# Expert rows written by plain scatters into a table of two rows for each token, in a two-layer hybrid step with 32 experts

## The chip, the cores and the metric

The kernel runs on one core of one Trainium2 chip. The metric is the device time of one execution in microseconds (us), given as the median over runs.

## What is computed

The program is one inference step of two trunk layers (an mLSTM and attention layer, then a state-space and delta-rule layer) over 128 prompt and 256 sample tokens of width 1024, all float32. Each layer ends in a mixture of experts, and only that part is touched by the change. Each of the T = 384 tokens chooses one of four expert groups, and two of the 8 experts in it. The result for a token is the sum of its two experts' outputs, each with its weight:

```
gsel = argmax(glog);  elog = elog[group gsel]
tv, ti = lax.top_k(elog, 2);  tw = softmax(tv) * gprob[gsel]
act_e = silu(x @ w_gate[e]) * (x @ w_up[e]) * combine[:, e]
y = sum over e of act_e @ w_down[e]
```

The reference evaluates all 32 experts on all tokens. Since the combine weights are zero but for two experts a token, 768 rows of expert output (2 x 384) carry all of the result.

## The kernel before

The five engines run programs written by hand, tied by named semaphores; S("name") is one. Work of TensorE (PE) stands in a fixed list of jobs, each with one of eight PSUM banks. computed(job) is the wait for its bank to be full, taken(job) the wait for it to be read.

**The expert stage** of a layer is gathered(l). Each expert has 64 slots (CAP), two experts share a pair of 128 slots, and there is one more pair with two spare blocks of 64, for experts that got over 64 tokens. That makes 17 pairs (PAIRS); the spare pair is the ninth in order (SPARE_AT = 8). For each pair, in the order of time:

- SyncE (SP) loads the weights of the two experts by 4 transfers of 1 MB for gate and up (load_pair, L595) and 2 of 1 MB for down (L600). There are two buffers. The gate and up weights of pair n are asked for when the gate-up products of pair n-2 are done, the down weights when its down products are done.
- GpSimd (POOL) gathers the tokens' rows by an indirect DMA from the DRAM table h_rows (gather, L736). The list of rows is slot_token, one column of 128 row numbers for each pair; an empty slot holds 512, which is out of bounds and moves nothing.
- PE turns the rows (L1167), ScalarE (ACT) copies them to SBUF (L1605), and PE multiplies them with gate and up (gate_up, L1180, 32 matmuls), 64 slots to each half of the array. ACT and VectorE (DVE) form silu(gate) * up (L1613, L2111), PE turns that (L1191), DVE copies it (L2115), and PE multiplies by down (L1205, 16 matmuls).
- ACT scales columns 0 to 511 of the result by the slots' weights (L1621), DVE columns 512 to 1023 (L2120), into one of two buffers yrow.
- POOL adds the 128 rows of yrow to the DRAM table y_rows of the layer by an indirect DMA with compute_op=ALU.add (scatter, L749). The row is the token's number, so that a token's two results meet in one row, in two different transfers. Each scatter waits until the one before has landed (semaphore gathered_scattered, L748). The spare pair's two blocks may hold the same token, so they go in two such transfers, with the lists spare_rows, which POOL copies out of slot_token ahead of the first gather (L756).

The tables y_rows, (T, D) for each layer, are filled with zeros near the start of the program by POOL (L719), after its list of small loads.

**Where the lists come from.** The router's tail on DVE makes hot_pair, which has a 1 where choice w of a token lies in pair q, and hot_row, which has a 1 at the slot within the pair. Products of the two on PE (slot_lists, L1140) give for each slot the token's number (hot_value 0, L2078) and its weight (hot_value 1, L2079). DVE writes them out as slot_token (L2084) and share (L2085). The bank is released by a small memset (L2087).

**The end of the stage.** SP waits for the last scatter, and reads the table back as three tiles of 128 tokens (ysel, L648, semaphores chosen0_in to chosen2_in). PE waits for all three and turns them by 24 transposes (L1262), after which DVE adds them to the residual (L1983). SP's next work, the weights of the second layer, stands behind the wait for the third tile. If more experts overflow than the spare blocks can hold, a dense path under overflow() runs all experts; it isn't taken here.

Of the kernel before, what the change touches and what calls it, by code (L numbers as in the profile page):

```python
# [90 lines left out]
C_ALL = C_TOKEN + TILES  # L91
NOWHERE = 512


def const_table():
# [21 lines left out]
    c[:, C_TOKEN:C_TOKEN + TILES] = row + P * np.arange(TILES)[None, :] - NOWHERE  # L117
    for parity in range(2):
        for half in range(2):
            for cond in range(2):  # L120
                c[32 * (2 * parity + half) + cond, C_SEL + 2 * parity + cond] = 1.0
# [126 lines left out]
def build(nc, a, o):  # L248
# [7 lines left out]
    with es:  # L256
# [12 lines left out]
        y_dram = [nc.dram_tensor(f"y_rows{l}", (T, D), F32).ap() for l in range(2)]  # L269
# [40 lines left out]
        pair_slot = cst[:, C_FIRST:C_FIRST + PAIRS + 1]  # L310
        iota, token = cst[:, C_IOTA:C_IOTA + P], cst[:, C_TOKEN:C_TOKEN + TILES]
# [8 lines left out]
        def scatters(l, n):  # L320

            return (PAIRS + 1) * l + n + 1 + (n >= SPARE_AT)
# [26 lines left out]
        spare_rows = sb("spare_rows", [P, 2], I32)  # L349
# [17 lines left out]
        def carve(n, at=None):  # L367
# [26 lines left out]
        act_n = [carve(FF) for _ in range(2)]  # L394
        act_s = [carve(2 * P).rearrange("p (j s) -> p j s", j=2) for _ in range(2)]
# [7 lines left out]
        hot_value = act_s[0].rearrange("p j s -> p (j s)")[:, 0:2 * TILES * 2 * PAIRS].rearrange(  # L403
            "p (w c n q) -> p w c n q", w=2, c=TILES, n=2)
        used[0] = base + 3 * 2 * T
        used[0] = max(used[0], work_end)
        ysel = carve(TILES * D).rearrange("p (c d) -> p c d", c=TILES)
# [123 lines left out]
        def _(sp):  # L531
# [92 lines left out]
            def moe(l):  # L624
# [21 lines left out]
                sp.wait_ge(S("gathered_scattered"), 16 * scatters(l, PAIRS - 1))  # L646
                for c in range(TILES):
                    sp.dma_start(ysel[:, c], y_dram[l][c * P:(c + 1) * P, :]).then_inc(S(f"chosen{c}_in"), 16)  # L648
# [10 lines left out]
            sp.wait_ge(S(f"chosen{TILES - 1}_in"), 16)  # L659
# [6 lines left out]
        def _(pool):  # L666
# [9 lines left out]
            with nc.allow_non_contiguous_dma(reason="small vectors"):  # L676
# [38 lines left out]
                last_token = pool.to_reg(T - 1)  # L715
# [1690 lines left out]
```

## Time and profile before

| | us |
|---|---|
| median of 3 runs | 1636.43 |
| the three runs | 1626.86, 1636.43, 1638.61 |
| the profiled execution | 1630.42 |
| its span | 1628.6 |
| PE busy | 1323.0 (81% of the span) |
| DVE, ACT, POOL busy | 522.8, 343.9, 153.8 |
| DMA, all queues | 335.48 MB, mean 206 GB/s |

The span is the time from the first to the last instruction, and the profiled execution is 1.8 us longer than that. PE is the busiest engine on the average, but the average mixes stages in which PE is the limit with stages in which it waits for weights. A row of the timeline gives start, duration, engine, line, operation and tiles, and in brackets the idle time ahead of it with what ended it. "issue" there means that the engine waited for something that the profile doesn't resolve to an instruction. A row of the windows gives for one stretch the busy time of each engine with its count of instructions, the TensorE clock that was granted (1.00 is 2.4 GHz, 0.50 is 1.2 GHz), the mean busy share of the 16 DMA engines, and the rate in GB/s. In the DMA view, q1 is the queue that SP issues to and q0 the one that POOL issues to; a row gives packets, MB, and the time that the packets took as a share of 16 engines over the stretch.

### The profile page before, as it was taken

What the parts mean: (1) busy time and instruction counts of PE and PEld (TensorE: products, weight loads), DVE (VectorE), ACT (ScalarE), POOL (GpSimd) and SP (SyncE); (2) the same over time, 40 slices, a digit from 0 to 9 for tenths busy, and PEclk for the clock granted to TensorE, in tenths of its full rate; (3) what the DMA queues carried; (4) which work ended last, traced back from release to release, by engine and by line L of the source; (5) the groups of instructions that cost most, each with busy time, mean ns of one, the idle gap of its engine ahead of it and who ended that gap; (6) DMA issues with size and microseconds to landing.
All of it is one profiled execution on the core that took longest, in us unless ns stands there. A gap on an engine that the chain in (4) does not pass through costs nothing.

```text
span 1628.6 us, 16057 instructions
## 1 busy us (share of the span) xinstructions
PE 1323.0 (81%) x6198; PEld 804.6 (49%) x6198; DVE 522.8 (32%) x1060; ACT 343.9 (21%) x720; POOL 153.8 (9%) x151
## 2 busy tenths in 40 slices
PE   5999899777977887877599997888869597878763
PEld 3545684344873333322366557787859533323223
DVE  3011662222242010000356816677741610000103
ACT  2100313322221111111326213222231211111102
POOL 2300000000011111110000010000000211111110
PEclk8999889877887998999799998999979699989986
DMA  9923555254444999997523200000033589999932
GB/s 338 320 71 120 190 172 207 89 221 155 181 177 185 409 412 406 396 397 279 163 73 134 76 3 1 27 1 1 1 122 163 206 312 409 406 402 397 391 148 78
DMA packets 81538, 335.48 MB, mean 206 GB/s; under 512 B 19160, under 2 KB 20354, under 8 KB 55217
## 3 DMA queue, kind: packets, MB, share of 16 engines
q1 hardware_dynamic: 67088, 309.94, 48.3%
q0 software_dynamic: 14368, 24.44, 5.8%
q8 instruction: 53, 0.87, 0.2%
q14 instruction: 29, 0.23, 0.0%
HBM read 329.96 MB, written 28.48 MB: 220 GB/s over the span
## 4 chain that ended last, share of the span: by engine, by line
PE 70%; DVE 14%; issue 10%; DMA 2%; ACT 2%; POOL 0%; SPq 0%; DVEq 0%; ACTq 0%; POOLq 0%
PE psum L867 19%; PE psum L1180 17%; PE psum L959 8%; PE psum L1205 8%; PE psum L891 3%; PE psum L1167 2%; PE psum L954 2%; DVE arena L2226 1%; DVE mix L2186 1%; PE psum L1080 1%; PE psum L1060 1%; PE psum L910 1%; PE psum L898 1%; PE psum L1191 1%; DVE arena L2115 1%
## 5 line engine op out<-in xcount | busy, mean ns | idle before, releaser
L1180 PE MATMUL psum<-arena 128*64 128x512 f32 x576 | 145.8, 664 | 41.6 <-issue 39.2
L1180 PE MATMUL psum<-ring,arena 128*64 128x512 f32 x512 | 134.1, 683 | 41.7 <-issue 41.7
L867 PE MATMUL psum<-hT,ring 128*128 128x384 f32 x448 | 150.9, 500 | 7.0 <-ACT hT L1461 5.1
L2111 DVE TENSOR_TENSOR arena<-arena,psum 128x256 f32<-128x256 f32 x34 | 14.3, 421 | 358.8 <-ACT arena L1613 358.8
L959 PE MATMUL psum<-ring 128*128 128x128 f32 x872 | 114.0, 289 | 18.4 <-issue 9.1
L867 PEld LDWEIGHTS psum<-hT,ring 128*128 128x128 f32 x448 | 87.5, 196 | 69.1 <-issue 12.1
L959 PEld LDWEIGHTS psum<-ring 128*128 128x128 f32 x872 | 108.2, 202 | 23.6 <-issue 13.8
L1180 PEld LDWEIGHTS psum<-arena 128*64 128x64 f32 x576 | 50.0, 153 | 136.2 <-issue 133.0
L867 PE MATMUL psum<-ring,hT 128*128 128x512 f32 (+2 forms) x336 | 116.4, 508 | 0.0
L1180 PEld LDWEIGHTS psum<-ring,arena 128*64 128x64 f32 x512 | 45.7, 157 | 129.8 <-issue 129.8
L1613 ACT ACTIVATE arena<-psum 128x256 f32<-128x256 f32 x34 | 13.0, 384 | 390.5 <-PE psum L1180 390.5
L867 PE MATMUL psum<-mix,ring 128*128 128x384 f32 x256 | 92.2, 517 | 0.0
L749 POOL DMA_INDIRECT y_rows<-arena,slot_token x32 | 50.6, 1582 | 416.7 <-DVE arena L2120 392.2
L867 PEld LDWEIGHTS psum<-ring,hT 128*128 128x128 f32 x336 | 58.5, 191 | 57.2 <-issue 56.4
L867 PEld LDWEIGHTS psum<-mix,ring 128*128 128x128 f32 x256 | 79.5, 316 | 6.3 <-issue 4.2
L1205 PE MATMUL psum<-arena 128*64 128x512 f32 x288 | 65.8, 598 | 9.3 <-DVE arena L2115 9.3
L2120 DVE TENSOR_SCALAR arena<-psum,share 128x512 f32<-128x512 f32 x34 | 25.5, 751 | 127.8 <-PE psum L1205 127.8
L1205 PE MATMUL psum<-ring,arena 128*64 128x512 f32 x256 | 58.5, 598 | 8.3 <-DVE arena L2115 8.3
L891 PE MATMUL psum<-ring,sil 128*32 128x512 f32 x384 | 57.3, 747 | 6.0 <-issue 6.0
L727 POOL TENSOR_TENSOR mix<-mix,arena 128x1024 f32<-128x1024 f32 x6 | 14.1, 2366 | 503.6 <-ACT mix L1595 503.6
L1983 DVE SCALAR_TENSOR_TENSOR xT<-psum,modT,xT 128x128 f32<-128x128 f32 x64 | 23.7, 413 | 109.1 <-PE psum L867 80.1
L2226 DVE SCALAR_TENSOR_TENSOR arena<-arena,colsT 128x388 f32<-128x388 f32 x80 | 49.8, 623 | 2.8
(475 smaller groups left out, 1654.7 us busy)
## 6 DMA issues: line engine op xcount, KB each, us to landing
ring<-in_ada_w SPq DMA_DIRECT2D x24, 2048.0 KB, 10.9
arena<-in_moe_w_gate SPq DMA_DIRECT2D x36, 1024.0 KB, 11.8
arena<-in_moe_w_up SPq DMA_DIRECT2D x36, 1024.0 KB, 14.3
arena<-in_moe_w_down SPq DMA_DIRECT2D x36, 1024.0 KB, 17.4
ring<-in_moe_w_gate SPq DMA_DIRECT2D x32, 1024.0 KB, 12.0
ring<-in_moe_w_up SPq DMA_DIRECT2D x32, 1024.0 KB, 17.9
ring<-in_moe_w_down SPq DMA_DIRECT2D x32, 1024.0 KB, 18.7
ring<-in_w_in_odd SPq DMA_DIRECT2D x7, 2048.0 KB, 7.9
```

The costliest lines, as they stand in the source:

```text
L749: pool.indirect_dma_start(out=y_dram[l], out_offset=bass.IndirectOffsetOnAxis(ap=where.bitcast(U32), axis=0), in_=yrow[u], in_offset=None, ...
L867: ins = mm(out, lhs(k), rhs(k), start=(k == 0), stop=(k == n - 1))
L891: ins = mm(b[at_:at_ + 32, :], sil[:, 4 * half + k, :], w[half][:, k, parity::2], start=(k == 0), stop=(k == 3), tile_position=(0, at_))
L898: ins = mm(b[:, 4 * m:4 * m + 4], mod_rows[:, m::4], pick, start=True, stop=True)
L954: ins = mm(b[:, tok(h)], col(h).to_broadcast([P, P]), ident, start=True, stop=True)
L959: ins = mm(b[:, h * width:(h + 1) * width], lhs(h), rhs(h), start=True, stop=True)
L1167: ins = nc.tensor.transpose(psum[:, k // 4, tok(k % 4)], hrow[q % 2][:, tok(k)], ident)
L1180: ins = mm(psum[half, 2 + s, :].rearrange("p (w f) -> p w f", w=2), hg[s][:, k, half], pair_gu[s][h][:, :, k, :], start=(k == 0), stop=(k ...
L1205: ins = mm(psum[half, 5 + n, :], act_s[s][:, j, half], pair_dn[s][h][:, j, 512 * n:512 * n + 512], start=(j == 0), stop=(j == 1), tile_pos ...
L1983: ins = stt(xT[:, m, t0:t1], bank(name, l, m)[:, t0:t1], modT[:, l, part, m, j:j + 1], xT[:, m, t0:t1], ALU.mult, ALU.add)
L2120: ts(yrow[q % 2][:, 512:D], psum[:, 6, :], share[:, ORDER[q]:ORDER[q] + 1], None, ALU.mult).then_inc(S(f"{kind}yb"), 1)
L2226: ins = stt(conv[:, i, :], cin[:, i, w:w + COUT], wcol[w], conv[:, i, :], ALU.mult, ALU.add)
```

## The change

The DRAM table y_rows of a layer gets two rows for each token, (2 * T, D): row token for its first choice, row T + token for its second. No two slots of any pair then write to the same row, and so the scatters no longer add and no longer wait for each other; each has a column of a new list, slot_row. The spare pair goes in one transfer like the others, and the copies into spare_rows are gone. slot_row comes from a third row of hot_value (one more DVE operation, and 51 columns in place of 34 in the product), with the constants C_ROW. It is written by a DVE operation that takes the place of the memset which released the bank. Scatters count on two semaphores, by the parity of the pair. At the end SP reads six tiles back, two for each 128 tokens. DVE adds the two tiles of each 128 tokens, and PE waits for these three sums. The zero fill is of twice as many rows.

```
-        y_dram = [nc.dram_tensor(f"y_rows{l}", (T, D), F32).ap() for l in range(2)]
+        y_dram = [nc.dram_tensor(f"y_rows{l}", (2 * T, D), F32).ap() for l in range(2)]
...
+    c[:, C_ROW:C_ROW + 2 * TILES] = row + P * np.arange(2 * TILES)[None, :] - NO_ROW
...
-            return (PAIRS + 1) * l + n + 1 + (n >= SPARE_AT)
+            return (PAIRS + 1 - n % 2) // 2 * l + n // 2 + 1
...
+        used[0] = base + 3 * 2 * T
+        ysel.append(carve(TILES * D).rearrange("p (c d) -> p c d", c=TILES))
...
-                sp.wait_ge(S("gathered_scattered"), 16 * scatters(l, PAIRS - 1))
+                for n in range(PAIRS - 2, PAIRS):
+                    sp.wait_ge(S(f"gathered_scattered{n % 2}"), 16 * scatters(l, n))
                 for c in range(TILES):
-                    sp.dma_start(ysel[:, c], y_dram[l][c * P:(c + 1) * P, :]).then_inc(S(f"chosen{c}_in"), 16)
+                    for w in range(2):
+                        at = w * T + c * P
+                        sp.dma_start(ysel[w][:, c], y_dram[l][at:at + P, :]).then_inc(S(f"chosen{c}_in"), 16)
...
-            sp.wait_ge(S(f"chosen{TILES - 1}_in"), 16)
+            sp.wait_ge(S(f"chosen{TILES - 1}_in"), 32)
...
-                    pool.dma_start(y_dram[l].rearrange("(p n) d -> p n d", p=P), bc(zero_row, 1, [P, T // P, D]))\
+                    pool.dma_start(y_dram[l].rearrange("(p n) d -> p n d", p=P), bc(zero_row, 1, [P, 2 * T // P, D]))\
...
+                        if n == 0:
+                            pool.wait_ge(*taken("ix", l))
                         pool.wait_ge(S("gathered_ya"), PAIRS * l + n + 1)
                         pool.wait_ge(S("gathered_yb"), PAIRS * l + n + 1)
-                        for i in range(2 if n == SPARE_AT else 1):
-                            where = spare_rows[:, i:i + 1] if n == SPARE_AT else slot_token[:, q:q + 1]
-                            if n + i:
-                                pool.wait_ge(S("gathered_scattered"), 16 * (scatters(l, n - 1) + i))
-                            pool.indirect_dma_start(
-                                out=y_dram[l], out_offset=bass.IndirectOffsetOnAxis(ap=where.bitcast(U32), axis=0),
-                                in_=yrow[u], in_offset=None, bounds_check=last_token,
-                                oob_is_err=False, compute_op=ALU.add).then_inc(S("gathered_scattered"), 16)
-
-                    for i in range(2):
-                        part = slice(CAP * i, CAP * i + CAP)
-                        nc.gpsimd.tensor_copy(spare_rows[part, i:i + 1], slot_token[part, PAIRS - 1:PAIRS]).then_inc(S("spare_rows"), 1)
-                    pool.wait_ge(S("spare_rows"), 2 * l + 2)
+                        pool.indirect_dma_start(
+                            out=y_dram[l], out_offset=bass.IndirectOffsetOnAxis(ap=slot_row[:, q:q + 1].bitcast(U32), axis=0),
+                            in_=yrow[u], in_offset=None, bounds_check=last_row,
+                            oob_is_err=False).then_inc(S(f"gathered_scattered{u}"), 16)
...
-                for c in range(TILES):
-                    pe.wait_ge(S(f"chosen{c}_in"), 16 * (l + 1))
+                pe.wait_ge(S("chosen_added"), TILES * (l + 1))
...
-                o_(tt(hot_value[:, :, :, 1, :], hot_pair, bc(wt, 3, each), ALU.mult))
+                tt(hot_value[:, :, :, 1, :], hot_pair, bc(wt, 3, each), ALU.mult)
+                o_(tt(hot_value[:, :, :, 2, :], hot_pair, bc(y_at, 3, each), ALU.mult))
...
-                take(v.memset(nbm, 0.0), "ix", l)
+                take(ts(slot_row[:], bank("ix", l)[:, 2 * PAIRS:3 * PAIRS], float(NO_ROW), None, ALU.add), "ix", l)
...
+                for c in range(TILES):
+                    dve.wait_ge(S(f"chosen{c}_in"), 32 * (l + 1))
+                    done(tt(ysel[0][:, c, :], ysel[0][:, c, :], ysel[1][:, c, :], ALU.add), "chosen_added")
```

On POOL, where the lists are ready and the first gathers go out, this stands before (the rows' add of shifts ends with L727, L736 is a gather):

```order
L727 TENSOR_TENSOR mix<-mix,arena 128x1024 [waits bank3_read,bank2_read]
L756 COPY spare_rows<-slot_token 64x1 [waits h_rows_out,rows_clear,slots,rows_zero]
L756 COPY spare_rows<-slot_token 64x1
L736 DMA arena<-h_rows,slot_token 128x1024 [waits spare_rows]
L736 DMA arena<-h_rows,slot_token 128x1024
```

and this after, where gathers are on L745 and scatters on L756:

```order
L736 TENSOR_TENSOR mix<-mix,arena 128x1024 [waits bank3_read,bank2_read]
L745 DMA arena<-h_rows,slot_token 128x1024 [waits h_rows_out,rows_clear,slots,rows_zero]
L745 DMA arena<-h_rows,slot_token 128x1024
L745 DMA arena<-h_rows,slot_token 128x1024 [waits gathered_turned]
L756 DMA y_rows<-arena,slot_row 768x1024 [waits gathered_yb,gathered_ya,bank6_read]
```

The two copies and the wait for them are gone, the first gather now stands right behind the waits for the list, and the first scatter waits for the bank that slot_row is read from.

On POOL, around the spare pair of the first layer, this stands before:

```order
L749 DMA y_rows<-arena,slot_token 384x1024 [waits gathered_scattered,gathered_yb,gathered_ya]
L736 DMA arena<-h_rows,slot_token 128x1024 [waits gathered_turned]
L749 DMA y_rows<-arena,spare_rows 384x1024 [waits gathered_scattered,gathered_yb,gathered_ya]
L749 DMA y_rows<-arena,spare_rows 384x1024 [waits gathered_scattered]
L736 DMA arena<-h_rows,slot_token 128x1024 [waits gathered_turned]
L749 DMA y_rows<-arena,slot_token 384x1024 [waits gathered_scattered,gathered_yb,gathered_ya]
```

and this after:

```order
L745 DMA arena<-h_rows,slot_token 128x1024 [waits gathered_turned]
L756 DMA y_rows<-arena,slot_row 768x1024 [waits gathered_yb,gathered_ya]
L745 DMA arena<-h_rows,slot_token 128x1024 [waits gathered_turned]
L756 DMA y_rows<-arena,slot_row 768x1024 [waits gathered_yb,gathered_ya]
L745 DMA arena<-h_rows,slot_token 128x1024 [waits gathered_turned]
```

One of the two transfers of the spare pair and every wait for an earlier scatter are gone; the order of gathers and scatters is the same.

On SP, at the end of the stage, where y_rows is read back, this stands before:

```order
L600 DMA arena<-in_moe_w_down 128x2048 [waits gathered_y1_computed]
L600 DMA arena<-in_moe_w_down 128x2048
L648 DMA arena<-y_rows 128x1024 [waits gathered_scattered]
L648 DMA arena<-y_rows 128x1024 x2
L527 TENSOR_LOAD flag [waits flag]
L527 ISA x2
L527 COMPARE_AND_BRANCH
```

and this after:

```order
L606 DMA arena<-in_moe_w_down 128x2048 [waits gathered_y1_computed]
L606 DMA arena<-in_moe_w_down 128x2048
L657 DMA arena<-y_rows 128x1024 [waits gathered_scattered0,gathered_scattered1]
L657 DMA arena<-y_rows 128x1024 x5
L533 TENSOR_LOAD flag [waits flag]
L533 ISA x2
L533 COMPARE_AND_BRANCH
```

Three loads have become six, in front of the same test for the overflow. On DVE, at the end of the router, this stands before (L2082 makes hot_row):

```order
L2076 SCALAR_TENSOR_TENSOR slots_f<-slots_f 128x6
L2078 TENSOR_TENSOR arena<-arena,cst 128x6x17
L2079 TENSOR_TENSOR arena<-arena,slots_f 128x6x17
L2082 TENSOR_SCALAR arena<-cst,slots_f 128x128 x6
L2084 TENSOR_SCALAR slot_token<-psum 128x17
L2085 COPY share<-psum 128x17
L2087 MEMSET small 128x2
```

and this after, where L2084 makes hot_row:

```order
L2077 SCALAR_TENSOR_TENSOR slots_f<-slots_f 128x6
L2079 TENSOR_TENSOR arena<-arena,cst 128x6x17
L2080 TENSOR_TENSOR arena<-arena,slots_f 128x6x17
L2081 TENSOR_TENSOR arena<-arena,cst 128x6x17
L2084 TENSOR_SCALAR arena<-cst,slots_f 128x128 x6
L2086 TENSOR_SCALAR slot_token<-psum 128x17
L2087 COPY share<-psum 128x17
L2089 TENSOR_SCALAR slot_row<-psum 128x17
```

One operation more stands ahead of the six that make hot_row, and the memset has become the one that writes slot_row.

## Rows read from the trace of the kernel before

**Rows 1.** The page's 40 slices of the span: DMA share in tenths.

```profile
DMA  9923555254444999997523200000033589999932
```

**Rows 2.** The chain that ended last, first layer's expert stage: start, us, what.

```profile
576.80 2.48 issue
579.27 8.75 PE psum L1180 x32
```

**Rows 3.** The same chain, end of that stage.

```profile
779.16 6.21 DMA y_rows<-arena,slot_token
...
785.75 0.43 SPq L648
786.23 5.17 DMA arena<-y_rows
...
791.64 5.36 PE psum L1262 x24
```

**Rows 4.** Windows of the first layer's expert stage.

```profile
512.30:540.00 27.70, 25.80 (x128) 10.29 (x130) 4.04 (x8) 5.60 (x8) 5.29 (x4) 1.00 0.98 385
...
574.00:608.00 34.00, 28.07 (x120) 10.60 (x118) 3.19 (x6) 4.19 (x6) 5.25 (x4) 0.90 1.02 409
```

**Rows 5.** Gate-up products (L1180) in the timeline of PE, first layer.

```profile
518.12 7.04 PE L1180 MATMUL psum<-ring,arena 128*64 128x512 f32 x32
...
530.61 7.04 PE L1180 MATMUL psum<-arena 128*64 128x512 f32 x32
...
562.66 8.52 PE L1180 MATMUL psum<-arena 128*64 128x512 f32 x32 [5.62 <-issue]
...
748.83 9.30 PE L1180 MATMUL psum<-ring,arena 128*64 128x512 f32 x32 [5.16 <-issue]
```

**Rows 6.** DMA queues, 512.3 to 748.8 us: packets, MB, share of 16 engines.

```profile
q1 hardware_dynamic: 12300, 89.63, 91.3%
q0 software_dynamic: 4176, 5.16, 8.7%
```

**Rows 7.** The same, second layer, 1311.3 to 1549 us.

```profile
q1 hardware_dynamic: 12297, 89.60, 90.7%
q0 software_dynamic: 4176, 4.96, 8.7%
```

**Rows 8.** POOL's queue while it moves gathers alone, 496 to 502 us.

```profile
q0 software_dynamic: 288, 0.32, 20.4%
...
arena<-h_rows,slot_token POOLq DMA_INDIRECT x3, 3.9
```

**Rows 9.** POOL's queue, 779 to 785.4 us, the last scatter of the first layer.

```profile
q0 software_dynamic: 144, 0.36, 41.3%
```

**Rows 10.** POOL's queue, 1447 to 1456 us, a spare block's scatter.

```profile
q0 software_dynamic: 144, 0.01, 1.6%
```

**Rows 11.** DMA issues of the whole span: KB each, us to landing.

```profile
y_rows<-arena,slot_token POOLq DMA_INDIRECT x32, 9.3
...
out_gdn<-arena POOLq DMA_DIRECT2D x2, 256.0 KB, 3.3
```

**Rows 12.** Timeline at the start of the stage.

```profile
491.58 0.26 DVE L2079 TENSOR_TENSOR arena<-arena,slots_f 128x102 f32<-128x102 f32 x1
...
495.09 0.18 DVE L2084 TENSOR_SCALAR slot_token<-psum 128x17 int32<-128x17 f32 x1 [1.95 <-PE psum L1140]
...
496.20 1.10 POOL L736 DMA_INDIRECT arena<-h_rows,slot_token  x1 [0.38 <-POOL spare_rows L756]
```

**Rows 13.** SP's queue, 785.3 to 791.5 us, y_rows read back.

```profile
q1 hardware_dynamic: 432, 1.57, 66.1%
```

**Rows 14.** An addition of 128x1024 on DVE, by form.

```profile
L2190 DVE TENSOR_TENSOR arena<-arena,mix 128x1024 f32<-128x1024 f32 x1 | 1.2, 1215 | 0.0
```

**Rows 15.** Windows around the zero fill.

```profile
66.00:81.00 15.00, 15.00 (x48) 8.82 (x47) 0.00 (x0) 1.47 (x3) 0.00 (x0) 1.00 1.00 390
81.00:90.00 9.00, 9.00 (x29) 5.16 (x28) 0.00 (x0) 0.98 (x2) 0.00 (x0) 1.00 0.03 10
```

More of the change, by code:

```diff
@@ L90 @@
 C_TOKEN = C_IOTA + P
-C_ALL = C_TOKEN + TILES
-NOWHERE = 512
+C_ROW = C_TOKEN + TILES
+C_ALL = C_ROW + 2 * TILES
+NOWHERE, NO_ROW = 512, 1024
 def const_table():
@@ L310, in build @@
         pair_slot = cst[:, C_FIRST:C_FIRST + PAIRS + 1]
+        y_at = cst[:, C_ROW:C_ROW + 2 * TILES].rearrange("p (w c) -> p w c", w=2)
         iota, token = cst[:, C_IOTA:C_IOTA + P], cst[:, C_TOKEN:C_TOKEN + TILES]
@@ L348, in build @@
         share = sb("share", [P, PAIRS])
-        spare_rows = sb("spare_rows", [P, 2], I32)
+        slot_row = sb("slot_row", [P, PAIRS], I32)
         spare_id = sb("spare_id", [1, 2, SPARE], I32)
@@ L394, in build @@
         act_n = [carve(FF) for _ in range(2)]
+        act_at = used[0]
         act_s = [carve(2 * P).rearrange("p (j s) -> p j s", j=2) for _ in range(2)]
@@ L713, in _ @@
                 zero_row = route[:].rearrange("p a c n -> p (a c n)")[:, 0:D]
-                last_token = pool.to_reg(T - 1)
+                last_token, last_row = (pool.to_reg(n - 1) for n in (T, 2 * T))
                 pool.wait_ge(S("zeroed"), 1)
                 for l in range(2):
-                    pool.dma_start(y_dram[l].rearrange("(p n) d -> p n d", p=P), bc(zero_row, 1, [P, T // P, D]))\
+                    pool.dma_start(y_dram[l].rearrange("(p n) d -> p n d", p=P), bc(zero_row, 1, [P, 2 * T // P, D]))\
                         .then_inc(S("rows_zero"), 16)
@@ L1139, in slot_lists @@
                     w_, c = n // TILES, n % TILES
-                    ins = mm(b[:, 0:2 * PAIRS], hot_row[:, w_, c, :], hot_value[:, w_, c].rearrange("p n q -> p (n q)"),
+                    ins = mm(b[:, 0:3 * PAIRS], hot_row[:, w_, c, :], hot_value[:, w_, c].rearrange("p n q -> p (n q)"),
                              start=(n == 0), stop=(n == 2 * TILES - 1))
@@ L1261, in moe @@
                     for c in range(TILES):
-                        ins = nc.tensor.transpose(b[:, tok(c)], ysel[:, c, m::KD], ident)
+                        ins = nc.tensor.transpose(b[:, tok(c)], ysel[0][:, c, m::KD], ident)
                     ready(ins)
@@ L1619, in gathered @@
                     if q >= 2:
-                        act.wait_ge(S(f"{kind}scattered"), 16 * scatters(l, q - 2))
+                        act.wait_ge(S(f"{kind}scattered{q % 2}"), 16 * scatters(l, q - 2))
                     fn(yrow[q % 2][:, 0:512], psum[:, 5, :], ACT.Copy, scale=share[:, ORDER[q]:ORDER[q] + 1]).then_inc(S(f"{kind}ya"), 1)
@@ L1754, in _ @@
             o_(v.memset(eps[:], EPS))
-            o_(v.memset(spare_rows[:], OOB))
             o_(v.memset(crowded[:, :, EXPERTS:EXPERTS + 1], 0.5))
@@ L2118, in gathered @@
                     if q >= 2:
-                        dve.wait_ge(S(f"{kind}scattered"), 16 * scatters(l, q - 2))
+                        dve.wait_ge(S(f"{kind}scattered{q % 2}"), 16 * scatters(l, q - 2))
                     ts(yrow[q % 2][:, 512:D], psum[:, 6, :], share[:, ORDER[q]:ORDER[q] + 1], None, ALU.mult).then_inc(S(f"{kind}yb"), 1)
@@ L2149, in dense @@
                 for c in range(TILES):
-                    dve.wait_ge(S(f"chosen{c}_in"), 16 * (l + 1))
-                    done(tt(ysel[:, c, :], ysel[:, c, :], yacc[:, c, :], ALU.add), f"{kind}merged")
+                    dve.wait_ge(S(f"chosen{c}_in"), 32 * (l + 1))
+                    done(tt(ysel[0][:, c, :], ysel[0][:, c, :], yacc[:, c, :], ALU.add), f"{kind}merged")
             def before_experts(l):
@@ L2171, in moe @@
                     dense(l)
+                for c in range(TILES):
+                    dve.wait_ge(S(f"chosen{c}_in"), 32 * (l + 1))
+                    done(tt(ysel[0][:, c, :], ysel[0][:, c, :], ysel[1][:, c, :], ALU.add), "chosen_added")
             before_experts(0)
```

6 lines of the change are left out of this document (3 added, 3 removed).

## Prediction

> **What bounds the kernel now.** I read the page's slices first: DMA stands at 9 tenths in two plateaus, the expert stages of the two layers [rows 1]. The page's busy times would point to PE, with 81% of the span, but the chain of waits in the plateau alternates between PE's products and gaps that the profile calls "issue" [rows 2]. What PE waits for there is told by the windows: the DMA share is 0.98 from 512.3 to 540 us and 1.02 from 574 to 608, at about 400 GB/s, two of seven windows in a row up to 744 us, which lie between 0.98 and 1.02 [rows 4]. The third check is the distance between pairs. Two early pairs whose weights were loaded ahead are 12.49 us apart (530.61 - 518.12). From pair 4 to pair 15, eleven steps later, it is (748.83 - 562.66) / 11 = 16.92 us [rows 5]. Where the granted clock of the window is 0.90, one pair's gate-up products take 8.75 us [rows 2]; where it is 1.00, 7.04 us [rows 4, 5]. So PE alone would need 12.49 + 1.7 = 14.2 us. So from gu_computed of the first pair (512.3 us) to the weights of pair 15 (748.8 us) the stage is as long as the work of the 16 DMA engines. The second layer has the same form, from 1311.3 to 1549 us [rows 7]. The last two pairs run at PE's own pace. Behind them stands a serial tail in which PE and DVE are idle: the last scatter takes 6.21 us from its issue to landing, the read-back some 6 us from its issue, and then come the 24 transposes [rows 3].
>
> So there are three places where this change can count: the DMA work of the plateau, the tail, and the start of the stage.
>
> **The plateau: adding against plain writes.** In the window 512.3 to 748.8 us (236.5 us), SP's queue moved 89.63 MB in 91.3% of the engines' time, that is 215.9 us, or 2.41 us for each MB [rows 6]. POOL's queue took 8.7%, or 20.6 us, for 5.16 MB; at 2.41 us for each MB those would be 12.4 us. The excess of 8.1 us is what small packets and the adding cost. The small packets are priced where POOL's queue moves almost no bytes: 144 packets took 1.6% of 9 us, 0.14 us, of which some 0.05 us are its 0.01 MB, so 0.1 us for about 141 small ones [rows 10]. The window has 4176 packets, of which 5.16 MB / 4096 B = 1260 are rows, so 2916 small ones, 2.0 us. That leaves 6.1 us for the adding. The second layer by the same steps (237.7 us): 215.6 us for 89.60 MB, 20.7 us for 4.96 MB, excess 8.8 us, less 2.1 us, 6.7 us [rows 7]. Two isolated stretches say the same in another way: gathers alone took 20.4% of 6 us for 0.32 MB, 3.8 us for each MB; the last scatter alone 41.3% of 6.4 us for 0.36 MB, 7.3 us for each MB [rows 8, 9]. An added row costs about two plain ones. Half of the 5.16 MB are scattered, 2.5 MB, so this second way gives (7.3 - 3.8) x 2.5 = 8.8 us. No row before shows an indirect plain write, so I keep 0 and 8.8 us for each layer as ends, and take 6.1 and 6.7, since they come from the busy window itself. Since the engines are full there, time that they save is time that the stage saves: 16.92 - 6.1 / 14, or 16.5 us a pair, is still over PE's 14.2. Sum: **-12.8 us**. The waits between scatters that go were not on the path: a scatter lands 9.3 us after its issue [rows 11], in a pair of 17 us. The second transfer for the spare pair is worth 0.14 us a layer, in the rounding.
>
> **The start.** slot_token is ready at 495.27 us, the first gather is issued at 496.20, behind the two copies [rows 12]; the 0.93 us fall to perhaps 0.15. One DVE operation of the form of L2079, 0.26 us, is added ahead of hot_row [rows 12], and 17 more columns in the product. The plateau starts from the first pair's products, so this counts: -0.8 + 0.3, -0.5 us for each layer (ends -0.9 and +0.3): **-1.0 us**. slot_row takes the memset's place, behind slot_token, beside the gather; behind the new wait of the first scatter (for the bank) only POOL's next gather is queued, and the bank is read some 20 us earlier.
>
> **The tail.** The last scatter: 6.21 us before [rows 3]. Its plain form has the nearest rows in a gather with 3.9 us [rows 8] and in plain writes to DRAM from POOL in a quiet stretch, 3.3 us [rows 11]. Ends: 3.3 and 6.2. I take 4.4, near the gather and somewhat over it since it is a write with a list: -1.8 us for each layer, **-3.6 us**. The Trainium skill ("DMA: Bandwidth & Descriptors", section "Anatomy of one DMA — SWDGE (gpsimd) path") says that a DMA from GpSimd has about 2 us of fixed time, mostly the receipt of its last write, and the rest goes by bytes. By that rule only the packets' own time would shrink, from 2.64 us to 1.4, so 1.3 us a layer in place of 1.8, and the sum would be -5.6 us; no row of before shows which holds.
>
> The read-back doubles: 432 packets took 66.1% of 6.2 us, 4.1 us for 1.57 MB [rows 13]. SP issues a load in 0.43 us [rows 3], less than the 1.3 us that 0.52 MB takes, so the bytes count in full: +4.1 us a layer, **+8.2 us** (ends 3.3 and 4.5 each). Then the sum of the last tile: an addition of 128x1024 takes 1.2 us [rows 14] with 0.1 for the semaphore, while the first two are done under the loads: +1.3 a layer, **+2.6 us**. Nothing hides this pair of terms, since PE waits for all three sums and SP's weights for the next layer for the loads. Those weights come 2.3 us later, against a chain that is 3.6 us later before they are needed, so they cost nothing more.
>
> **The zero fill** moves 3.1 MB more, 7.6 us of all engines at 2.41 us for each MB. It stands behind the small loads on its queue, and after it the engines are nearly idle: share 0.03 from 81 to 90 us, while PE is busy in all of both windows [rows 15]. These 8.7 free us take it, so 0; with that cover gone it would be 7.6 us, once.
>
> **Sum.** -12.8 - 1.0 - 3.6 + 8.2 + 2.6 = -6.6 us. The span goes from 1628.6 to 1622.0, the profiled execution from 1630.4 to 1623.8. The median of the runs is 6.0 us over the profiled execution, and the runs spread over 11.8 us, twice the effect. I set the number off the mean of the four executions shown, 1633.1: 1626.5, rounded to 1627.
>
> **Rivals.**
>
> *The adding is nearly free, and row traffic as such is the cost.* If a packet of a scattered row takes its time because of the list and the two ends in different memories, the plateau keeps its length, and so does the last scatter. Then the doubled read-back and the sums decide: -1.0 + 8.2 + 2.6 = +9.8 us, 1643: slower than before. The point is where the plateau and the last scatters together save less than 9.8 us. For it: POOL's queue takes more per MB in gathers too, 3.8 us against SP's 2.41 [rows 6, 8]. Against it: the ratio of 1.9 between scatter and gather in isolated stretches [rows 8, 9].
>
> *PE takes the bound.* If with shorter waits the granted clock stays at its lower level for more pairs, PE's pace of 14.2 us a pair would still be below 16.5, so some of the gain at most is lost in the pairs behind the last weights, where a gate-up product takes 9.30 or 7.04 us [rows 5]. Some 2 us a layer: net -2.6 us, 1631.
>
> *All ends fall well.* Plateau -17.6, start -1.8, last scatters -5.8, read-back +6.6, sums +2.4: -16.2 us, 1617. For it: the second way of pricing. Against it: that way takes scatters in an idle stretch, where an engine also waits for answers from memory.
>
> *The zero fill isn't hidden*: +7.6 us on top of the forecast, net +1.0, 1634. Against it stands the free stretch [rows 15].
>
> **How the numbers follow.** Forecast (net -12 to -3 us) 0.55; PE's clock takes a part 0.12; all ends well 0.13; adding nearly free 0.12; zero fill 0.08. A measurement of this kernel can tell about 1%, 16 us, from no change. Only the case of good ends comes near that on the fast side, and the spread of the runs can carry it over; the slow side needs two of the bad cases at once. Faster by over 1%: 0.11, within 1%: 0.84, slower: 0.05. The range takes in the cases and the runs' spread: 1616, just under the good ends, 1642 for nearly the rival on the slow side. The forecast's own range, as medians go, is 1620 to 1632.
>
> **What would show it.** In the plateau POOL's queue should take 6% of the engines' time in place of 8.7 at the same MB, and both plateaus should be 6 to 7 us shorter, at a DMA share still near 1.0 and pairs 16.5 us apart. The last scatter should land in 4 to 5 us. From the read-back's issue to its landing it should take some 10 us, then one addition of 1.2 us, then the transposes. The stretch from 81 to 89 us should be full of writes with PE still busy. The prediction is wrong if the plateau keeps its length, or if the DMA share falls well below 1 in it (another limit took over), or if PE waits for weights between 90 and 110 us.

## The result: 1637.5 us before, 1616.7 us after

With three more runs the median of the kernel before is 1637.52 us (6 runs), and that of the changed kernel is 1616.65 us (1612.7 to 1621.15, 6 runs). The ratio is 0.9874, with a 95% interval from 0.9845 to 0.9904. The forecast was 1627 with a net gain of 6.6 us. The time lies inside the range given (1616 to 1642) by 0.65 us, but the gain is 20.9 us, three times the forecast, and beyond its own range (1620 to 1632). That it landed inside is luck more than insight: the forecast gave a gain of over 1% a chance of 0.11, and the gain is 1.3%. It also started from 1633.1 us, the mean of the four executions at hand, and the median of six is 1637.5. The profiled execution takes 1612.70 us with a span of 1610.9, against 1630.42 and 1628.6: 17.7 us less.

Where the 17.7 us went is read from a few marks in the two traces. The plateau is counted here from the start of the first pair's gate-up products to the start of pair 15's. "Read-back" runs from SP's first issue to the start of PE's transposes.

| us | before, layer 0 and 1 | after, layer 0 and 1 | change | forecast |
|---|---|---|---|---|
| up to the first pair | 502.8 | 503.7 | +0.9 | -0.5 |
| plateau | 246.0, 246.1 | 234.9, 234.9 | -22.3 | -12.8 |
| pair 15 to the last scatter's issue | 30.3, 32.1 | 29.7, 29.7 | -3.0 | 0 |
| last scatter, issue to SP's next issue | 6.2, 5.9 | 4.0, 3.5 | -4.6 | -3.6 |
| read-back, and the addition after | 6.3, 6.7 | 11.7, 11.8 | +10.5 | +10.8 |
| transposes to the next layer's first pair | 511.3 | 512.4 | +1.0 | -0.5 |
| after the last transposes' start | 34.8 | 34.6 | -0.2 | 0 |

One row carries most of the difference of 11.1 us: the plateaus gained 9.5 us more. The tail came out nearly as forecast.

The two stretches ahead of the plateaus (2.9 us over the forecast together) and the last pairs (3.0 us under it) cancel. Of the 1.9 us that those two stretches grew, 0.88 and 1.03 us lie ahead of the first operation that the edit touches, L2078 before and L2079 after (491.39 and 1290.96 us before, 492.27 and 1284.37 after). What comes so early moves from one execution to the next: in three executions of the changed kernel the first pair starts at 503.7, 508.1 and 510.2 us.

The gate-up products in the timeline of PE, changed kernel, first layer (the rows for comparison are [rows 5]):

```profile
503.74 9.12 PE L1183 MATMUL psum<-arena 128*64 128x512 f32 x32 [1.17 <-ACT arena L1607]
...
543.70 7.04 PE L1183 MATMUL psum<-ring,arena 128*64 128x512 f32 x32
...
560.34 9.82 PE L1183 MATMUL psum<-arena 128*64 128x512 f32 x32 [3.99 <-issue]
```

and for the end of the plateau:

```profile
738.63 8.78 PE L1183 MATMUL psum<-ring,arena 128*64 128x512 f32 x32 [2.52 <-issue]
...
754.10 7.09 PE L1183 MATMUL psum<-arena 128*64 128x512 f32 x32 [1.08 <-issue]
```

Pair 3 no longer waits at all (7.04 us with no bracket), and from pair 4 to pair 15 the distance is (738.63 - 560.34) / 11 = 16.21 us, where it was 16.92.

Windows of the changed kernel in the plateau, with the columns of [rows 4]:

```profile
540.00:574.00 34.00, 28.76 (x126) 10.63 (x128) 3.35 (x7) 4.52 (x7) 4.04 (x4) 0.90 1.02 422
574.00:608.00 34.00, 27.83 (x126) 10.56 (x122) 3.94 (x7) 4.88 (x7) 4.04 (x4) 0.95 1.01 422
...
676.00:710.00 34.00, 28.89 (x126) 10.88 (x124) 3.20 (x6) 4.19 (x6) 4.04 (x4) 0.90 1.00 412
```

The DMA share is what it was, the rate is 422 GB/s in place of 409. DMA still sets the pace, with more weights in the same time. The DMA queues in the first plateau of the changed kernel, 512.8 to 738.6 us (before: [rows 6]):

```profile
q1 hardware_dynamic: 12181, 88.77, 94.2%
q0 software_dynamic: 4032, 5.15, 6.3%
```

and in the second, 1305 to 1531.2 us (before: [rows 7]):

```profile
q1 hardware_dynamic: 12175, 88.72, 94.1%
q0 software_dynamic: 4032, 4.95, 6.0%
```

POOL's queue takes 6.3% and 6.0% for 5.15 and 4.95 MB, where it took 8.7%. That is the 6% that the forecast named: 14.2 us in place of 20.6 in the first layer, 6.4 us less. Yet the plateau is 11.1 us shorter. The share is a mean over 16 engines, and the mean doesn't hold the whole saving. Nor does a mean of 1.0 say that no engine idles: windows with 1.02 show more packet time than there is time, so packets of one engine overlap in this count.

The tail of the first layer in the timeline of the changed kernel, POOL's scatter, SP's six loads, DVE's three additions, PE's transposes:

```profile
768.35 0.98 POOL L756 DMA_INDIRECT y_rows<-arena,slot_row  x1 [12.75 <-DVE arena L2122]
772.33 3.02 SPq L657 DMA_DIRECT2D arena<-y_rows  x6
777.57 1.23 DVE L2176 TENSOR_TENSOR arena<-arena 128x1024 f32<-128x1024 f32 x1 [9.98 <-DMA arena<-y_rows]
780.31 1.23 DVE L2176 TENSOR_TENSOR arena<-arena 128x1024 f32<-128x1024 f32 x1 [1.51 <-DMA arena<-y_rows]
...
782.74 1.22 DVE L2176 TENSOR_TENSOR arena<-arena 128x1024 f32<-128x1024 f32 x1 [1.20 <-DMA arena<-y_rows]
...
784.02 4.65 PE L1264 MATMUL psum<-cst,arena 128*128 128x128 f32 x24 [17.22 <-DVE arena L2176]
```

The scatter takes 3.98 us from its issue to SP's next (772.33 - 768.35), near the 4.4 taken. The loads run from 772.33 to 782.7, the last addition takes 1.22 us on the path as forecast, and the first two lie under the loads. POOL's queue from 768 to 772.3 us, the last scatter, with the columns of [rows 9]:

```profile
q0 software_dynamic: 144, 0.36, 22.1%
```

and SP's queue from 772.3 to 782.8 us, the read-back, with the columns of [rows 13]:

```profile
q1 hardware_dynamic: 864, 3.15, 79.4%
```

The scatter's packets took 22.1% of 4.3 us, 0.95 us in place of 2.64 for the same 0.36 MB; the read-back's 79.4% of 10.5 us, 8.3 us for 3.15 MB, twice 4.1.

The zero fill, windows with the columns of [rows 15]:

```profile
66.00:81.00 15.00, 15.00 (x49) 8.77 (x48) 0.00 (x0) 1.47 (x3) 0.00 (x0) 1.00 1.03 404
81.00:90.00 9.00, 9.00 (x29) 5.32 (x28) 0.00 (x0) 0.85 (x2) 0.00 (x0) 1.00 0.85 344
90.00:97.00 7.00, 7.00 (x17) 3.04 (x17) 0.55 (x1) 0.13 (x1) 0.00 (x0) 1.00 0.86 300
```

The share from 81 to 90 us is 0.85 in place of 0.03, and PE is busy in all of the three windows. The idle stretch took the fill.

The start of the stage, with the columns of [rows 12]:

```profile
492.63 0.26 DVE L2081 TENSOR_TENSOR arena<-arena,cst 128x102 f32<-128x102 f32 x1
...
496.16 0.18 DVE L2086 TENSOR_SCALAR slot_token<-psum 128x17 int32<-128x17 f32 x1 [1.98 <-PE psum L1143]
...
497.18 1.08 POOL L745 DMA_INDIRECT arena<-h_rows,slot_token  x1 [12.72 <-DVE slot_token L2086]
```

The first gather comes 0.84 us behind the end of slot_token (496.34), 0.78 us in the second layer, where it came 0.93 us behind with the two copies between. The forecast had 0.15. The first of the two copies had indeed started 0.13 us behind slot_token (495.40 against 495.27), but a gather in its place doesn't.

### The profile page after: what moved, and what is told of

Its sections match the earlier page's. It is cut to its first block, busy times and chain, and to the rows that moved or that the text cites. A ratio compares the mean times of both kernels' runs of the same rounds, so it can differ in the third digit from the quotient of the medians.

```text
span 1610.9 us, 16071 instructions
## 1 busy us (share of the span) xinstructions
PE 1317.4 (82%) x6198; PEld 804.4 (50%) x6198; DVE 530.8 (33%) x1067; ACT 343.9 (21%) x720; POOL 129.4 (8%) x145
## 4 chain that ended last, share of the span: by engine, by line
PE 70%; DVE 14%; issue 9%; DMA 2%; ACT 2%; SPq 0%; POOL 0%; DVEq 0%; ACTq 0%; POOLq 0%
PE psum L870 19%; PE psum L1183 17%; PE psum L962 8%; PE psum L1208 8%; PE psum L894 3%; PE psum L1170 2%; PE psum L957 2%; DVE arena L2231 1%; DVE mix L2191 1%; PE psum L1083 1%; PE psum L1063 1%; PE psum L901 1%; DMA arena<-y_rows 1%; PE psum L913 1%; PE psum L1194 1%
## 5 line engine op out<-in xcount | busy, mean ns | idle before, releaser
L1183 PE MATMUL psum<-arena 128*64 128x512 f32 x576 | 153.1, 692 | 45.9 <-issue 43.6
L1183 PE MATMUL psum<-ring,arena 128*64 128x512 f32 x512 | 119.8, 622 | 19.4 <-issue 19.4
L962 PE MATMUL psum<-ring 128*128 128x128 f32 x872 | 114.8, 290 | 17.7 <-issue 8.4
L870 PEld LDWEIGHTS psum<-hT,ring 128*128 128x128 f32 x448 | 88.3, 198 | 69.7 <-issue 12.8
L1208 PE MATMUL psum<-arena 128*64 128x512 f32 x288 | 65.8, 598 | 9.3 <-DVE arena L2117 9.3
L756 POOL DMA_INDIRECT y_rows<-arena,slot_row x34 | 34.1, 1003 | 459.9 <-DVE arena L2122 430.3
L1208 PE MATMUL psum<-ring,arena 128*64 128x512 f32 x256 | 58.5, 599 | 8.3 <-DVE arena L2117 8.3
L736 POOL TENSOR_TENSOR mix<-mix,arena 128x1024 f32<-128x1024 f32 x6 | 14.1, 2369 | 509.1 <-ACT mix L1597 509.1
```

Source lines behind the costliest of these rows:

```text
L756: pool.indirect_dma_start(out=y_dram[l], out_offset=bass.IndirectOffsetOnAxis(ap=slot_row[:, q:q + 1].bitcast(U32), axis=0), in_=yrow[u], ...
L870: ins = mm(out, lhs(k), rhs(k), start=(k == 0), stop=(k == n - 1))
L962: ins = mm(b[:, h * width:(h + 1) * width], lhs(h), rhs(h), start=True, stop=True)
L1183: ins = mm(psum[half, 2 + s, :].rearrange("p (w f) -> p w f", w=2), hg[s][:, k, half], pair_gu[s][h][:, :, k, :], start=(k == 0), stop=(k ...
L1208: ins = mm(psum[half, 5 + n, :], act_s[s][:, j, half], pair_dn[s][h][:, j, 512 * n:512 * n + 512], start=(j == 0), stop=(j == 1), tile_pos ...
```

## The experiments

Theory A, formed from the result and from the packets: the plateau goes at the pace of the fullest of the 16 DMA engines. It supposes that a transfer of weights gives each engine an equal part and has landed when all have done it, while the rows of a gather or a scatter aren't spread equally: the slots of an expert are filled from the first on, 24 of 64 on the average (768 rows over 32 experts), so the engines that own the first partitions of each half would carry the most rows.

The packet records of the plateau hold 1255 rows of 4096 B on POOL's queue in either kernel. Before, they fall into two groups, at 159 and at 327 ns; in the changed kernel nearly all take 159 ns. So a gathered or plainly scattered row takes 159 ns at the median, an added one 327, and by theory A the adding cost 168 ns for each row of the fullest engine, not of the mean one. Theory B keeps the forecast's mean, and puts the rest on the waits between scatters; C puts all on those waits; D says that the places of the rows don't matter.

The times of the experiments are medians; each plateau is counted as above and comes from one profiled execution. Three executions of the changed kernel have plateaus from 234.4 to 234.9 us, so a difference of 1 us says little and one of 3 us counts.

| | median us | ratio to before, 95% | plateaus us |
|---|---|---|---|
| kernel before | 1637 to 1639 | | 246.0, 246.1 |
| changed kernel | 1616.65 | 0.9874 [0.9845, 0.9904] | 234.9, 234.9 |
| e1_add_back | 1646.33 | 1.0044 [1.0016, 1.0073] | 246.3, 246.6 |
| e2_serial_back | 1617.64 | 0.9871 [0.9834, 0.9908] | 234.8, 235.6 |
| e3_spread | 1604.02 | 0.9791 [0.9753, 0.9828] | 231.2, 228.6 |
| e4_crowd | 1646.30 | 1.0051 [1.0025, 1.0077] | 249.8, 248.2 |
| c1_control | 1620.57 | 0.9895 [0.9822, 0.9967] | 234.5, 234.8 |
| e5_before_spread | 1615.22 | 0.9878 [0.9824, 0.9932] | 237.4, 235.7 |
| e6_one_table | 1609.61 | 0.9850 [0.9801, 0.9899] | 234.7, 234.4 |
| e7_no_fill | 1618.94 | 0.9900 [0.9869, 0.9931] | 234.7, 234.5 |
| e8_spread_again | 1607.33 | 0.9814 [0.9779, 0.9849] | 231.4, 229.9 |
| c2_control | 1622.05 | 0.9898 [0.9864, 0.9932] | 234.6, 234.4 |

### The adding alone, put back

```
-                            oob_is_err=False).then_inc(S(f"gathered_scattered{u}"), 16)
+                            oob_is_err=False, compute_op=ALU.add).then_inc(S(f"gathered_scattered{u}"), 16)
```

> The changed kernel with one edit: its scatters add again (compute_op=ALU.add), into rows that are zero and that nobody else writes. No wait comes back. Theory A (the fullest DMA engine sets the plateau, and an added row takes 327 ns of it where a plain one takes 159): both plateaus, from the first pair's gate-up products to the start of pair 15's, grow by some 11 us each to about 246 us, as they were before (246.0 and 246.1 against 234.9 and 234.9), and the last scatter of a layer takes some 6 us again in place of 4.0. That is about +26 us on the changed kernel's 1616.7, so 1640 to 1645, slower than the kernel before by the doubled read-back. Rival B (the adding costs its mean over 16 engines, 6.4 us a layer, and the rest of the gain came from the waits between scatters): +6 to +7 us in each plateau, 1633. Rival C (all of it came from the waits): +0 in the plateaus.

Measured: 1646.33 us, +29.7 on the changed kernel, and the plateaus back at 246.3 and 246.6 us, as long as before. In the timeline of PE of this kernel, the first pair's gate-up products:

```profile
510.11 8.90 PE L1183 MATMUL psum<-arena 128*64 128x512 f32 x32 [1.17 <-ACT arena L1607]
```

and those of pair 15, 246.34 us later:

```profile
756.45 8.61 PE L1183 MATMUL psum<-ring,arena 128*64 128x512 f32 x32 [3.56 <-issue]
```

POOL's queue in this plateau (519 to 756.4 us):

```profile
q0 software_dynamic: 4032, 5.16, 8.6%
```

The mean share is 8.6%, about as in [rows 6], where it was 8.7%. Against 6.3% in the changed kernel this prices the adding at 20.4 - 14.2 = 6.2 us, while the plateau grew by 11.4. The last scatter of the first layer takes 5.94 us, from 786.85 to SP's issue at 792.79:

```profile
786.85 1.55 POOL L756 DMA_INDIRECT y_rows<-arena,slot_row  x1 [13.04 <-DVE arena L2122]
```

The plateaus (+23.1 us) and the last scatters (about +2 each) make most of the 29.7. So the whole of the plateau's gain is the adding. B's 6 to 7 us and C's 0 are out.

### The waits alone, put back

```
+                        if n:
+                            pool.wait_ge(S(f"gathered_scattered{1 - u}"), 16 * scatters(l, n - 1))
                         pool.indirect_dma_start(
```

> The changed kernel with one edit: each scatter again waits on POOL until the one before has landed. They stay plain. Theory A: nothing, within 2 us of the changed kernel's 1616.7, since a scatter lands in some 8 us of a pair of 16 us. Rival B: +4 to +5 us in each plateau, 1626. Rival C: +11 us in each plateau, 1638.

Measured: 1617.64 us, plateaus of 234.8 and 235.6. The series in which the scatters stood cost nothing that shows: 0.7 us in one plateau, 0 in the other.

### The places of the slots

```
-    c[:, C_IOTA:C_IOTA + P] = np.arange(P)
+    slot = np.arange(P)
+    place_of = 64 * (slot // 64) + 4 * (slot % 8) + slot % 64 // 8 % 4 + 32 * (slot % 64 // 32)
+    c[:, C_IOTA + place_of] = slot
```

This is e3_spread. hot_row compares with iota, so the constant alone decides in which partition a slot's row, weight and target lie. For e4_crowd the line in the middle reads:

```
+    place_of = 64 * (slot // 64) + 4 * (slot % 64 // 8) + slot % 8 % 4 + 32 * (slot % 8 // 4)
```

> The changed kernel with one constant changed: slot r of an expert's 64 lies in another of its 64 partitions, 4 * (r % 8) + r // 8 % 4 + 32 * (r // 32), so that consecutive slots fall on eight different DMA engines, if partition p belongs to engine 8 * (p >> 6) + ((p >> 2) & 7). That is the assignment that the Trainium skill gives ("DMA: Bandwidth & Descriptors", section "The descriptor swizzle"). An expert has 24 rows on the average, and its slots are filled from the first one on, so as it stands the first engine of a half gets 4 to 8 rows of each transfer and the last often none. The routing of these inputs gives for the first 14 pairs of layer 0 and 1 at most 68 and 72 rows on one engine, at a mean of 38 and 42; the new places give 45 and 49. Theory A (the fullest engine sets the pace): 23 rows less on it, each gathered and scattered at 159 ns, 7.3 us less in each plateau, 227.5 us; 1602. Rival D (the mean over the engines sets the pace, or rows go to engines in turn): no change, 1616.7, or a few us more.

> The changed kernel with the same constant changed the other way: eight consecutive slots fall on one engine, place 4 * (r // 8) + r % 8 % 4 + 32 * (r % 8 // 4). The fullest engine then has 108 and 107 rows in the first 14 pairs in place of 68 and 72, at the same mean. Theory A: 40 and 35 rows more at 2 x 159 ns, +12.7 and +11.1 us in the plateaus, about 1640. Rival D: no change, 1616.7.

Measured: spreading gives 1604.02 us with plateaus of 231.2 and 228.6, crowding 1646.30 us with 249.8 and 248.2. The instructions, bytes and packets are the same in both. Gate-up products in the timeline of the spread kernel, of the first pair and of pair 3:

```profile
509.94 9.08 PE L1185 MATMUL psum<-arena 128*64 128x512 f32 x32 [1.17 <-ACT arena L1609]
...
549.85 7.04 PE L1185 MATMUL psum<-ring,arena 128*64 128x512 f32 x32
```

and of pair 15:

```profile
741.11 9.54 PE L1185 MATMUL psum<-ring,arena 128*64 128x512 f32 x32 [4.37 <-issue]
```

The same in the timeline of the crowded kernel, the first pair and pair 3, which waits 1.37 us here and not at all in the spread one:

```profile
506.70 8.97 PE L1185 MATMUL psum<-arena 128*64 128x512 f32 x32 [1.17 <-ACT arena L1609]
...
548.04 7.09 PE L1185 MATMUL psum<-ring,arena 128*64 128x512 f32 x32 [1.37 <-issue]
```

and pair 15:

```profile
756.53 8.65 PE L1185 MATMUL psum<-ring,arena 128*64 128x512 f32 x32 [3.08 <-issue]
```

The DMA queues in the first plateau of the spread kernel, 519 to 741.1 us:

```profile
q1 hardware_dynamic: 12041, 87.75, 94.5%
q0 software_dynamic: 4032, 5.15, 6.4%
```

and of the crowded one, 515.8 to 756.5 us:

```profile
q1 hardware_dynamic: 12364, 90.13, 91.4%
q0 software_dynamic: 4032, 5.15, 5.9%
```

POOL's 5.15 MB take 14.2 us of mean engine time in both (6.4% of 222.1, 5.9% of 240.7), and the plateaus differ by 18.7 us. D is out: the mean can't show on which engines the rows lie. The shares of both queues together are 97.3% in the crowded plateau and 100.9% in the spread one, which fits engines that idle more in the crowded one. The sizes fit A roughly. Crowding was to add 12.7 and 11.1 us and added 14.9 and 13.3; spreading was to take 7.3 each and took 3.7 and 6.3. For the part that spreading didn't bring, no run shows the cause.

The rule used for the places is the Trainium skill's ("DMA: Bandwidth & Descriptors", section "The descriptor swizzle"), which gives engine 8 * (p >> 6) + ((p >> 2) & 7) for partition p in a transfer to all 128 partitions. The signs of both runs agree with it for an indirect DMA as well, the sizes within a fifth for crowding and at half to nine tenths for spreading. The packet records don't name the engine of a packet, so the runs show that the partitions matter in this pattern, and that the limit is the DMA engine and not something else shared by the same partitions is argued.

### The same places in the kernel before

The same constant in the kernel before, with its adding scatters in series.

> The kernel before, with adding scatters in series, and only the slots' places changed as in e3_spread. Theory A (the rows on the fullest DMA engine set the plateau, an added one for 327 ns and a plain one for 159): the spread kernel's plateaus of 231.2 and 228.6 us, plus the adding on the fullest engine after spreading, 45 and 49 rows x 168 ns = 7.6 and 8.2 us: 238.8 and 236.8, in place of 246. So 7 to 9 us less in each layer than the kernel before, 1637.5 - 16 = 1621. Rival D (the mean sets the pace): no change, 1637. Rival B (the serial scatters hold something up): no change either, since the waits stay.

Measured: 1615.22 us, with plateaus of 237.4 and 235.7, against 238.8 and 236.8 expected. The first pair's gate-up products in its timeline:

```profile
510.97 8.94 PE L1182 MATMUL psum<-arena 128*64 128x512 f32 x32 [1.17 <-ACT arena L1607]
```

and those of pair 15:

```profile
748.40 9.69 PE L1182 MATMUL psum<-ring,arena 128*64 128x512 f32 x32 [4.09 <-issue]
```

One constant in the kernel before brings as much as the whole change: the intervals of the two ratios, 0.9878 and 0.9874, lie over each other. Its plateaus are 1 to 3 us longer than the changed kernel's, and its tail is shorter, as it reads one table back. It also shows that the price of the adding hangs on the places: with the slots filled from the front the adding costs 11.4 and 11.7 us (e1_add_back against the changed kernel), with the slots spread 6.2 and 7.1 us (this kernel against e3_spread, where the waits differ too, which cost nothing above). A mean over the engines has no room for that; theory A had 7.6 and 8.2 us for the spread places.

### The tail, and the fill

e6_one_table, in short:

```
-                    for w in range(2):
+                    for w in range(1):
...
-                pe.wait_ge(S("chosen_added"), TILES * (l + 1))
+                for c in range(TILES):
+                    pe.wait_ge(S(f"chosen{c}_in"), 16 * (l + 1))
...
-                    done(tt(ysel[0][:, c, :], ysel[0][:, c, :], ysel[1][:, c, :], ALU.add), "chosen_added")
```

> The changed kernel, but it reads back only the first table of each layer, three tiles, and leaves out the second experts' outputs and the three additions on DVE. This times the tail: the forecast's +4.1 us for the doubled read-back and +1.3 us for the last addition, for each layer. If they are right, the time from the last scatter's issue to PE's transposes falls from 15.67 to about 10.3 us in layer 0, and the total by 10.8 us to 1606. Rival: the loads of the second table were partly hidden, and the total falls by less than 6 us.

Measured: 1609.61 us, 11.0 us less than the control of its group (1620.57), whose four executions lie between 1606.76 and 1625.96 us, so the traces say more than this difference. The tail of the first layer in the timeline:

```profile
768.94 0.97 POOL L756 DMA_INDIRECT y_rows<-arena,slot_row  x1 [12.09 <-DVE arena L2123]
773.41 1.28 SPq L657 DMA_DIRECT2D arena<-y_rows  x3
...
780.11 5.20 PE L1265 MATMUL psum<-cst,arena 128*128 128x128 f32 x24 [12.73 <-DMA arena<-y_rows]
```

From the last scatter's issue to the transposes it is 780.11 - 768.94 = 11.17 us, 4.5 less than 15.67. From SP's first issue alone it is 6.70 us, 5.0 less than 11.69. In the second layer the time from pair 15 to the transposes falls from 45.0 us (46.5 in the control) to 39.7, by 5.4 at least. The forecast had 5.4 us a layer for the second table and its addition; measured are 4.5 and 5.4 in the profiled executions, and 5.5 a layer in the medians. The rival, loads of the second table that were partly hidden, had under 6 us in both layers together and is out.

e7_no_fill:

```
-                for l in range(2):
-                    pool.dma_start(y_dram[l].rearrange("(p n) d -> p n d", p=P), bc(zero_row, 1, [P, 2 * T // P, D]))\
-                        .then_inc(S("rows_zero"), 16)
...
-                    pool.wait_ge(S("rows_zero"), 32)
...
-                dve.wait_ge(S("rows_zero"), 32)
```

> The changed kernel without the zero fill of the tables (nothing is left out of the result: each token of these inputs has both its rows written). If the fill is hidden in the idle stretch behind the small loads, as the forecast has it: no change, 1617 within 3 us. Rival: the fill, 6.3 MB, delays weights or holds the clock: 8 to 15 us less, about 1605.

Measured: 1618.94 us, 1.6 under its control, well inside the spread. The share from 81 to 90 us is 0.00 (the changed kernel had 0.85), and PE is as busy as with the fill:

```profile
66.00:81.00 15.00, 15.00 (x48) 8.81 (x47) 0.00 (x0) 1.47 (x3) 0.00 (x0) 1.00 0.53 178
81.00:90.00 9.00, 9.00 (x28) 5.13 (x27) 0.00 (x0) 0.98 (x2) 0.00 (x0) 1.00 0.00 0
```

### The spread kernel against the changed one

> The spread kernel of e3 once more, on one chip with the changed kernel (c2_control), to set a number on what it gains over it. The plateaus of e3 were 3.7 and 6.3 us shorter than those of the changed kernel, and theory A has 7.3 each. So 10 to 15 us less than the control. If the places of the slots mattered little, the two would be within 3 us.

> The changed kernel itself, so that the other kernels of this group have it on the same chip: about 1617, plateaus of 235 us.

> The changed kernel itself: 1617 to 1620 us, plateaus of 234.5 to 235 us.

Measured: 1607.33 us with the spread places, 1622.05 for the changed kernel on the same chip, 14.7 us or 0.9% less. The plateaus are 3.2 and 4.5 us shorter than the control's, 7.7 us of the 14.7; in the profiled executions, which lie 22 us apart, the stretch between the two stages is another 5.3 us shorter (510.5 us in place of 515.7) and the first pair starts 9.5 us earlier (500.7 in place of 510.2), neither of which the edit touches. So the gain that can be laid to the slots is nearer 8 us than 15, and theory A had 14.6. All six executions of the spread kernel (1600.04 to 1609.84 us) lie below all six of the control (1619.75 to 1623.06). The intervals of the ratios to the kernel before are less clear: 0.9753 to 0.9828 and 0.9779 to 0.9849 for the spread kernel, 0.9845 to 0.9904, 0.9822 to 0.9967 and 0.9864 to 0.9932 for the changed one.

## Why the forecast was right, and where it wasn't

- **The plateau as the bound**: right. Its length followed the DMA work in every experiment, while PE's work was the same.
- **The price of the adding**: this is the term that was mis-sized. The step read "since the engines are full there, time that they save is time that the stage saves", and took 6.1 and 6.7 us from the mean share of 16 engines. The mean was right: POOL's queue fell from 20.6 to 14.2 us in the first layer. The stage, however, saved 11.1 and 11.2 us, which is what theory A gives the fullest engine. By the routing of these inputs and the rule of places, 68 and 72 rows lie on that engine in the first 14 pairs, whose scatters fall before pair 15; at 168 ns each that makes 11.4 and 12.1 us. The share of 0.98 to 1.02 in [rows 4] had hidden this, as it is a mean.
- **The 16.5 us a pair** followed from the same step; it is 16.21.
- **The waits in series cost nothing**: right, shown by e2_serial_back.
- **The start**: wrong; it gained nothing. -1.0 us was forecast, with the first gather 0.15 us behind slot_token. From the start of L2078 to the first gate-up products it is 11.44 us before (502.83 - 491.39) and 11.47 after (503.74 - 492.27). Taking the copies away left 0.84 us between slot_token and the gather, 0.09 us less than with them.
- **The last scatter**: -3.6 us forecast, -4.6 measured. The value of 4.4 us was a little high (3.98 and 3.54). The Trainium skill's rule ("DMA: Bandwidth & Descriptors", section "Anatomy of one DMA — SWDGE (gpsimd) path") gave -1.3 us a layer from the packets alone; measured are -2.2 and -2.4. The trace's packet records take the first layer's scatter apart. From its issue to its first row it was 2.12 us and is 1.54 (POOL's issue itself fell from 1.55 to 0.98); the stretch from the first row's start to the last row's end was 3.76 us and is 1.88; from there to SP's next issue it was 0.34 us and is 0.56. In the second layer the three are 2.12, 3.48 and 0.34 before, 1.53, 1.29 and 0.72 after. So outside the rows there were 2.46 us before and 2.10 and 2.25 after, near the rule's 2 us, but that part shrank too, and most of it lies ahead of the first row and not behind the last one. The rows shrank by 1.9 and 2.2 us at the same bytes, more than I had put in.
- **The read-back and the addition**: +10.8 forecast, +10.5 measured, and e6_one_table takes them off again.
- **The zero fill at nothing**: right, shown twice, by the windows and by e7_no_fill.
- **The rivals**: "the adding is nearly free" is refuted by e1_add_back. "All ends fall well" had -17.6 us for the plateaus, and even that end, from the isolated stretches, was below the 22.3 measured. So the range of this term left out the true value, and the time fell inside the total range only since the spread of the runs was in it. That case as a whole came to 1617 us, as measured, by other terms than those that happened: its start gained 1.8 us and its read-back with the addition cost 9.0, where the start gained nothing and the read-back cost 10.5.
- Not forecast: the last two pairs are 3.0 us faster in the two layers together. In the second layer their gate-up products took 8.55 and 8.78 us before and 7.09 and 7.09 after. The granted clock over these two was 0.83 and 0.81 before and 1.00 after. e1_add_back has both lengths in one layer (8.61 and 7.09), so I lay nothing on it.

## What to carry to other kernels

Where the DMA share is near 1 and the traffic is uneven, ask which engine is the fullest, as a saving here counted by the rows on that engine. The mean saving was forecast to a tenth (6.1 us, measured 6.4), and the stage saved 11.1. In a gather or scatter of partly filled lists, the place of the filled slots is free to choose, and here one constant in the kernel before was worth as much as the whole change. And a change that takes a cost off a full resource may pay for a longer tail: here 22 us of plateau for 11 us of read-back and addition.

## What the runs showed of the hardware

In the plateau a row of 4096 B takes a DMA engine 159 ns by a plain packet, in either direction, and 327 ns where it is added to DRAM; the last scatter alone, with nothing beside it, had added rows of 328 ns at the median and 465 ns on the average. The indirect DMA with adding also takes POOL longer to issue, 1.55 us against 0.98. The time of a stage full of DMA hangs on the partitions in which the rows of its gathers and scatters lie: with bytes, packets and mean engine time of these rows the same, two orders of the slots made plateaus of 231.2 and 249.8 us. The first gather of a stage starts 0.84 and 0.78 us behind the instruction that releases it; what fills that time, no run shows.
